# Modulation in pairs of column groups, the past turned a tile ahead, and the projection's first inputs loaded in the setup

## The reference

```python
def adaln(c, w, b):
    mod = jax.nn.silu(c) @ w + b                     # c: prompt's and sample's vector, w: 1024 x 3072
    shift, scale, gate = jnp.split(mod, 3, axis=-1)
    return shift[:, None, :], scale[:, None, :], gate[:, None, :]
...
hn = rmsnorm(x, a_g_norm) * (1 + scale) + shift      # 1024 columns
q_a, c_new, kr_new, mq, mk, mv, mi, mf, mo, z = split_cols(h @ w_in, IN_A_SIZES)
...
c_all = jnp.concatenate([c_past.astype(dt), c_new], axis=1)      # the past: 1024 latents of 256, rope part of 32
kv = jnp.einsum('bsc,chd->bshd', c_all, w_kv_b)                  # keys and values of 8 heads
```

## Time and profile before

| | us |
|---|---|
| median of 3 runs | 3859.77 (3858.14 to 3865.64) |
| the profiled execution, its own time | 3865.66 |
| its span | 3864.1 |
| TensorE busy | 3622.8 |
| VectorE busy | 1685.9 |
| ScalarE busy | 1067.2 |
| GpSimd busy | 401.0 |

### The profile page before, as it was taken

How to read it: one execution, slowest core, us unless ns; L and a number is a source line. 1 busy time by engine, 2 the same in 40 slices (tenths; PEclk the granted TensorE clock), 3 DMA queues, 4 the chain that set the end, 5 groups by cost and what they waited for, 6 DMA issues and landing times. The chain is left out here.

```text
span 3864.1 us, 46030 instructions
## 1 busy us (share of the span) xinstructions
PE 3622.8 (94%) x17237; PEld 2138.7 (55%) x17237; DVE 1685.9 (44%) x2976; ACT 1067.2 (28%) x2758; POOL 401.0 (10%) x555
## 2 busy tenths in 40 slices
PE   7899999999988999989997699999999988799998
PEld 3455555555435666765553355555554568666765
DVE  2122222222225555555553344344444448477784
ACT  0211211211124444541111133232231345322322
POOL 0000000000000000000000101000000011344441
PEclk9899999999967999998998799999999998799999
DMA  5712212221154100004332411121111139855552
GB/s 181 246 49 77 74 59 65 74 65 59 41 137 118 30 20 25 15 12 164 109 101 85 176 47 54 51 67 45 50 51 41 56 113 254 240 164 148 158 156 74
DMA packets 349537, 362.14 MB, mean 94 GB/s; under 512 B 129652, under 2 KB 277855, under 8 KB 347167
## 3 DMA queue, kind: packets, MB, share of 16 engines
q1 hardware_dynamic: 307302, 305.44, 26.5%
q10 hardware_dynamic: 35112, 30.37, 2.6%
q0 software_dynamic: 6928, 23.73, 2.1%
HBM read 231.45 MB, written 128.01 MB: 93 GB/s over the span
## 5 line engine op out<-in xcount | busy, mean ns | idle before, releaser
L523 PE MATMUL a_bank<-a_w_in,a_hT 128*128 128x512 f32 (+4 forms) x1904 | 754.2, 554 | 2.2 <-ACT a_hT L612 2.2
L1872 PE MATMUL d_bank<-d_hT,d_w_in 128*128 128x512 f32 (+1 forms) x1920 | 722.5, 532 | 7.9 <-DMA d_w_in<-in_c_w_in 4.4
L523 PEld LDWEIGHTS a_bank<-a_w_in,a_hT 128*128 128x128 f32 (+1 forms) x1904 | 351.6, 187 | 367.5 <-issue 316.6
L1872 PEld LDWEIGHTS d_bank<-d_hT,d_w_in 128*128 128x128 f32 x1920 | 337.9, 193 | 351.2 <-issue 338.5
L976 PE MATMUL c_ps<-c_kT,c_q 96*128 96x512 f32 (+5 forms) x688 | 303.9, 576 | 32.7 <-ACT c_prob L1114 15.2
L2693 PE MATMUL r_bank<-k_w_next,r_mixT 128*128 128x512 f32 (+1 forms) x544 | 252.6, 615 | 2.1 <-ACT r_mixT L2751 2.1
L1878 PE MATMUL d_bank<-d_w_in,d_hT 128*128 128x344 f32 (+3 forms) x816 | 245.2, 455 | 0.0
L2005 DVE SCALAR_TENSOR_TENSOR d_cv<-d_xb,k_wconv,d_cv 128x512 f32<-128x512 f32 (+1 forms) x360 | 236.9, 658 | 12.8
L1434 PE MATMUL m_bank<-m_w_out,m_mixT 128*128 128x512 f32 (+1 forms) x544 | 237.3, 594 | 0.7 <-ACT m_mixT L1522 0.7
L2003 DVE TENSOR_SCALAR d_cv<-d_xb,k_wconv 128x512 f32<-128x512 f32 (+1 forms) x120 | 52.9, 441 | 397.6 <-ACT d_xb L1945 383.6
L976 PEld LDWEIGHTS c_ps<-c_kT,c_q 96*128 96x128 f32 (+1 forms) x688 | 125.0, 199 | 163.5 <-issue 130.0
(11 more groups left out here) (361 smaller groups left out, 4306.9 us busy)
## 6 DMA issues: line engine op xcount, KB each, us to landing
k_n_kv<-scratch_qkv SPq DMA_DIRECT2D x17, 1024.0 KB, 5.2
scratch_qkv<-d_ts SPq DMA_DIRECT2D x64, 256.0 KB, 2.3
a_w_ada<-in_c_w_ada SPq DMA_DIRECT2D x16, 768.0 KB
d_w_in<-in_c_w_in ACTq DMA_DIRECT2D x6, 2048.0 KB, 21.1
l_kT<-scratch_g_kT SPq DMA_DIRECT2D x17, 512.0 KB, 5.2
l_qT<-scratch_g_qT SPq DMA_DIRECT2D x17, 512.0 KB, 5.9
k_n_kT<-scratch_g_kT SPq DMA_DIRECT2D x17, 512.0 KB, 5.9
r_qT<-scratch_g_qT SPq DMA_DIRECT2D x17, 512.0 KB, 8.0
```

The source lines that it names most:

```text
L523: mm = nc.tensor.matmul(o[:n, 0:w], hT[u][:, k, :n], w_in[:, k, c0:c0 + w], start=(k == 0), stop=(k == KD - 1))
L1872: mm = nc.tensor.matmul(o[:, 0:w.w], w_in[:, k, w.a * P:(w.a + 1) * P], hT[w.r % 2][:, k, 0:w.w], start=(k == 0), stop=(k == KD - 1))
```

## The change

`Modulation.rows` writes quarter q to partitions 32q and 32q+1 of one PSUM bank and alternates between the two quarters of a half within each k; `row_done` is raised once per half, and both copies follow it. The same alternation is made in "ada": 256 columns become two groups of 128, on partitions 0 and 32, and VectorE adds the two groups separately.

In `Past`, the three PSUM banks and the turned latent are doubled. The transposes are a method of their own (`turn`), called one tile ahead; so are VectorE's two copies of their result (`turned_to`). The transposes of tile t wait for `k_out` of tile t-2, the products of tile t also for `v_out` of tile t-2. The hand-written order becomes: tiles 0 to 3, `rows(0)`, 4 and 5, `rows(1)`, 6, `turn`, 7.

The first two tiles of x and the "latent" part of the weights are tensors of their own, kept over both phases. The setup loads them on SyncE's queue, behind the modulation's weights and ahead of the zero stores, and waits for them at its end; project_a no longer loads or waits for them, and its parts are mlstm, gate0, gate1.

```diff
 class Modulation:
+        for k in range(KD):
+            for q in (2 * j, 2 * j + 1):
+                mm = nc.tensor.matmul(self.ps_row[32 * q:32 * q + 2, :], self.K["silu_c"][:, k:16:KD],
                                       self.w[j][:, k, q % 2 * 512:(q % 2 + 1) * 512],
                                       start=(k == 0), stop=(k == KD - 1))
+        mm.then_inc(self.row_done, 1)
...
 class Past:
+    def turn(self, pe, t):
+        nc, ident, pst = self.nc, self.K["consts"][:, 0, :], self.pst[t % 2]
+        if t == 0:
+            pe.wait_ge(self.c_in, 32)
+        if t >= 2:
+            pe.wait_ge(self.k_out, t - 1)
+        for k in range(2):
+            nc.tensor.transpose(pst[:, k * P:(k + 1) * P], self.c[:, t, k * P:(k + 1) * P], ident)
+        nc.tensor.transpose(pst[:DR, 256:256 + P], self.kr[:, t, :], ident).then_inc(self.turned, 1)
+
     def tensor(self, pe, t):
         if t == 0:
             pe.wait_ge(self.w_in, 64)
+            self.turn(pe, 0)
+        if t + 1 < NP:
+            self.turn(pe, t + 1)
+        pe.wait_ge(self.turned_out, t + 1)
+        if t >= 2:
+            pe.wait_ge(self.v_out, t - 1)
+            pe.wait_ge(self.k_out, t - 1)
...
     def vector(self, dve, t):
         if t == 0:
             self.ch = Chain(dve, self.own)
+            self.turned_to(dve, 0)
+        if t + 1 < NP:
+            self.turned_to(dve, t + 1)
...
 def setup
             mod.load(sp, io["a_w_ada"])
+            for u in range(2):
+                sp.dma_start(K[f"a_x{u}"][:, :], io["x_prompt"][u * P:(u + 1) * P, :]).then_inc(first_in, 16)
+            for dst, c0, n in ((0, 0, C_G), (C_G, D_G, 8)):
+                sp.dma_start(K["a_lat"][:, :, dst:dst + n], io["a_w_in"][:, c0:c0 + n].rearrange("(k p) n -> p k n", p=P)).then_inc(first_in, 16)
...
             sp.wait_ge(pad_stored, 16 * 6)
+            sp.wait_ge(first_in, 16 * 4)
...
 def project_a
                     for k in range(KD):
-                        mm = nc.tensor.matmul(o[0:2, 0:CA + CC], K["silu_c"][:, k:16:KD], w_ada[u][:, k, :],
-                                              start=(k == 0), stop=(k == KD - 1))
+                        for g in range(2):
+                            mm = nc.tensor.matmul(o[32 * g:32 * g + 2, 0:P], K["silu_c"][:, k:16:KD],
+                                                  w_ada[u][:, k, g * P:(g + 1) * P], start=(k == 0), stop=(k == KD - 1))
                     mm.then_inc(done, 1)
```

More of the change, by code:

```diff
@@ L182, in store @@
         sp.wait_ge(self.st_k, 16 * NP)
+    def turn(self, pe, t):
[7 more added lines that the diff above has]
+        nc.tensor.transpose(pst[:DR, 256:256 + P], self.kr[:, t, :], ident).then_inc(self.turned, 1)
     def tensor(self, pe, t):
-        nc, ident = self.nc, self.K["consts"][:, 0, :]
+        nc, psv, psk, cT = self.nc, self.psv[t % 2], self.psk[t % 2], self.cT[t % 2]
         if t == 0:
             pe.wait_ge(self.w_in, 64)
[L188 to L191, removed]
-        for k in range(2):
[L193 to L197, removed]
+            self.turn(pe, 0)
[5 more added lines that the diff above has]
+            pe.wait_ge(self.k_out, t - 1)
+        for k in range(2):
+            mm = nc.tensor.matmul(psv[:, :], cT[:, k, :], self.wv[:, k, :], start=(k == 0), stop=(k == 1))
         mm.then_inc(self.v_done, 1)
@@ L290, in _ @@
             nc.tensor.transpose(ps_vec[:, 128:224], crow[:, :], ident[0:96, 0:96]).then_inc(cols_done, 1)
-            for t in range(2):
+            for t in range(4):
                 past.tensor(pe, t)
@@ L294, in _ @@
             mod.rows(pe, 0)
-            for t in range(2, 5):
+            for t in range(4, 6):
                 past.tensor(pe, t)
             mod.rows(pe, 1)
-            past.tensor(pe, 5)
+            past.tensor(pe, 6)
             mod.turn(pe)
-            for t in range(6, NP):
-                past.tensor(pe, t)
+            past.tensor(pe, 7)
         @block.vector
@@ L311, in _ @@
             nc.vector.tensor_tensor(K["silu_c"][:, :], tc[:, :], K["cols"][:, 0:16], ALU.mult).then_inc(silu_done, 1)
-            for t in range(2):
+            for t in range(4):
                 past.vector(dve, t)
             mod.rows_out(dve, 0)
-            for t in range(2, 5):
+            for t in range(4, 6):
                 past.vector(dve, t)
             mod.rows_out(dve, 1)
-            past.vector(dve, 5)
+            past.vector(dve, 6)
             mod.finish(dve)
-            for t in range(6, NP):
-                past.vector(dve, t)
+            past.vector(dve, 7)
         @block.gpsimd
@@ L366, in project_a @@
         wv = sb("wv", [P, 2, H * DV])
-        x = [sb(f"x{u}", [P, D]) for u in range(2)]
+        x = [K[f"a_x{u}"] for u in range(2)]
         xn = sb("xn", [P, D])
@@ L391, in project_a @@
         bank = [ctx.enter_context(nc.psum_tensor(f"a_bank{i}", [P, 512], F32)) for i in range(4)]
-        PARTS = {"latent": (C_Q, C_G), "mlstm": (C_MQ, C_MO), "gate0": (C_MO, C_Z + 512), "gate1": (C_Z + 512, W_A)}
+        PARTS = {"mlstm": (C_MQ, C_MO), "gate0": (C_MO, C_Z + 512), "gate1": (C_Z + 512, W_A)}
         part_in = {name: sem(f"{name}_in") for name in PARTS}
-        part_dmas = {name: 32 if name == "latent" else 16 for name in PARTS}
         weights_in = sem("weights_in")
@@ L425, in _ @@
                 if name in names[2:]:
-                    sp.wait_ge(part_in[names[names.index(name) - 2]], part_dmas[names[names.index(name) - 2]])
+                    sp.wait_ge(part_in[names[names.index(name) - 2]], 16)
                 if name == "gate1":
@@ L430, in _ @@
                 s0 = D_MQ if name == "mlstm" else c0
[L431 to L434, removed]
+                sp.dma_start(w_in[:, :, c0 - C_MQ:c1 - C_MQ],
+                             io["a_w_in"][:, s0:s0 + c1 - c0].rearrange("(k p) n -> p k n", p=P)).then_inc(part_in[name], 16)
             def load_ada(t, u):
@@ L521, in proj @@
                 o, done = claim(name, t)
+                weights, at = (w_lat, c0) if c0 < C_MQ else (w_in, c0 - C_MQ)
                 for k in range(KD):
-                    mm = nc.tensor.matmul(o[:n, 0:w], hT[u][:, k, :n], w_in[:, k, c0:c0 + w],
+                    mm = nc.tensor.matmul(o[:n, 0:w], hT[u][:, k, :n], weights[:, k, at:at + w],
                                           start=(k == 0), stop=(k == KD - 1))
@@ L528, in loaded @@
                 if isinstance(t, int) and t == 0:
-                    pe.wait_ge(part_in[name], part_dmas[name])
+                    pe.wait_ge(part_in[name], 16)
             turn_x(0)
@@ L535, in body @@
                 pe.wait_ge(hT_done, 2 * (t + 1))
-                loaded(t, "latent")
                 proj(t, u, "qa", C_Q, QL)
@@ L599, in square_x @@
                 n = rows(t)
-                act.wait_ge(x_in[u], 16 * (i + 1))
+                if later(i):
+                    act.wait_ge(x_in[u], 16 * i)
                 nc.scalar.activation(junk[:n, :], x[u][:n, :], ACT.Square, scale=float(D) ** -0.5,
@@ L2999, in build @@
                 K[n] = K[n][:, :]
-            run(setup, project_a)
+            with ExitStack() as early:
+                keep(early, {"a_x0": [P, D], "a_x1": [P, D], "a_lat": [P, KD, C_MQ]})
+                run(setup, project_a)
             keep(first, {**{"m_" + n: [P, T1, MH] for n in ("lf", "lt", "cum", "tot", "w", "M", "prev", "mend", "pend")},
```

56 lines of the change are left out of this document (28 added, 28 removed).

## The result

The changed kernel takes 3806.43 us (median of 4 runs, 3794.88 to 3806.94) against 3861.9 us of the kernel before in the same comparison: ratio 0.9849, 95% interval 0.9828 to 0.9871. The forecast was 3803.3 us, within 3795 to 3816, and faster. The profiled execution took 3806.93 us, its span is 3805.3 us.

A forecast was written before the change was run, and what follows sets the result against it. TensorE was taken to bound the projection's loop, with latencies and waits for VectorE in and after the setup. Savings of 21.6 + 27.3 + 7.6 = 56.5 us from 3859.8 gave 3803.3 us, range 3795 to 3816.

The forecast's parts named there:

- Pairs in the loop: First projection's loop: alternating two column groups saves 1.71 us of modulation in each of 16 tiles, 27.3 us.
- Pairs in the setup: Setup's modulation: alternating column groups cuts each half to 6.85 us; the two halves save 13.7 us.
- Turns ahead: Setup's past tiles: transposes a tile ahead take the latent copy off the path, 5.74 us a tile; setup keeps 7.9 us.
- The layout: Predicted setup timeline from the first key copy at 25.20 us, tile 1 at low clock, to the last store at 78.0.
- x and the weights: Projection's head: loading x and the latents' weights in the setup brings TensorE's first product 7.6 us earlier.
- The second part of the weights: First projection: lands near 118, wanted at 123.6; if it shares the engines evenly, 128.3, losing 4.7 us.
- Rival 1: Setup and loop modulation: pairs overlap only in part, 1.59x; 46 us saved, 3813.6 us; chance 0.10.
- 2: Rival on setup and loop modulation: pairs don't overlap at all; 15.5 us saved, 3844 us; chance 0.04.
- rival 4: Setup and loop modulation: each column-group switch waits for the record before; 79 us slower, 3938 us; chance 0.02.
- Rival 3: Setup's end: SyncE's queue runs the past's stores late, setup gives nothing; 34.9 us remain, 3825 us; chance 0.04.
- The sum: Whole kernel: setup 21.6, loop 27.3 and projection's head 7.6 give 56.5 us saved.

The follow-up runs named there:

- e1: The changed kernel with the loop's per-tile modulation back in one column group (16 records of 256 columns): 3828.92 us, ratio 0.9926.
- e2: The changed kernel with the same column groups run one after the other instead of alternating, in setup and loop: 3832.88 us, ratio 0.9929.
- e4: The changed kernel with the past's transposes and VectorE's copies of them back in their own tile: 3814.84 us, ratio 0.9893.
- e7: The kernel of e5 with the setup's modulation in one pass alternating between four column groups, after tile 4: 3798.47 us, ratio 0.9841.
- e5: The changed kernel with transposes waiting on a semaphore for VectorE's copies from their own bank, no longer for key copies: 3797.65 us, ratio 0.9841.
- e9: The kernel of e7 with six zero stores moved behind the projection's first loads, reading from a cleared table: 3792.18 us, ratio 0.9822.
- e8: The changed kernel with the loop's per-tile modulation in four column groups of 64 columns: 3786.65 us, ratio 0.9813.

## Why the prediction was right, point by point

- **Pairs in the loop** (27.3 us forecast): 57.00 us a tile before (174.57 to 231.58), 55.31 after, 1.70 x 16 = 27.2. The pace read from the attention's value product held for groups of 2 columns as for 64. e1 takes it away alone; e2 shows that the alternation carries it.
- **Pairs in the setup** (13.7): two times 13.90 - 7.04 = 13.7.
- **Turns ahead** (7.9): together with the pairs 23.35 instead of 21.6 us, so 9.65. Here the number is in part luck. Two slow tiles of the kernel before are gone, each worth 1.7 us: tile 1, which I had left at the low clock and held in my range, and tile 3, which I had not seen. The layout has the new tile 3 at the high clock, so 1.7 of the forecast 7.9 us came from the clock unnamed and only 6.2 from the look-ahead. Measured are 3.4 us from the clock and 6.8 from the look-ahead, less 0.5 us for the first key copy, which came at 25.69 instead of 25.20. A tile took 5.62 against 5.74, and the look-ahead also hides the halves' joined copies (e4), which I did not name. In the ten profiles of kernels that turn a tile ahead no tile behind tile 0 ran at the low clock; in the two that turn in the tile two did each (1 and 3 before, 3 and 7 in e4). That points at the shorter waits, but no run shows it. When the first tile begins is chance: at 18.66 here, 17.11 before, and between 16.70 (e4) and 19.11 (e2) over all profiles.
- **x and the weights** (7.6): 7.9. The second part of the weights had landed by 94.08 and was wanted at 99.93, so nothing was lost there.
- **Rival 1** (part overlap) and 2 fell at 7.04 and 1.92 us: the halves became 1.97 times as fast, not 1.59; rival 4 with them. **Rival 3** (the store queue) was 13 us away from deciding: the past's first store went out at 51.38 instead of 49, and stores with a backlog took 1.0 us each where I had taken 0.6, so it was cleared at 63.4, not by 60. In e7, where TensorE ends the setup's work 14.5 us sooner (60.2 against 74.8), it decided.
- **The sum** of 56.5 was 58.3 at the attention's start, 58.8 in the spans and 55.5 in the medians. The first is the one to read: the stages behind differ by some 13 us from profile to profile, and it is chance that they were equal here (2765.9 before, 2765.4 after).

## What to carry to other kernels

A product with few output columns on TensorE can be cut into column groups at 32-partition steps of one bank, with the group as the innermost loop; look for a place in the same trace where that is done already and take its pace. When such a cut, or a finer semaphore, frees an engine in a short phase, ask next which queue ends the phase: here the finer semaphore paid at once (e5), but the pass over four groups only once the zero stores were moved out of the setup (e7, e9).

## What the hardware showed that I had not expected

- Four column groups run fully side by side: 64 records of 512 columns in 7.05 us (e7), where two groups take 7.04 us for 32, and of 64 columns in 1.08 us, a start every 0.014 us with a weight load for each (e8).
- TensorE mixes records of two column groups across about four records of its instruction order (e2), 1.7 us at the seam of a half and 0.4 us at that of the loop's product.
